# Attention: the table addition and the row maximum as one VectorE operation on negated scores, and the second block's attention in one unrolled pass

## The chip, the cores and the metric

The kernel runs on one core of one Trainium2 chip. The metric is the device time of one execution in microseconds (us); a lower time is better.

## The reference

The program computes two transformer blocks, one after the other, on 512 tokens of width 1024. Only the attention parts matter here.

The first block has four attention variants ("mixers") side by side, each with 4 heads: moba, mla, dil (dilated) and swa (sliding window with a sink). At 512 tokens each comes down to dense causal attention with its own table of biases and masks. The second block has a layer of attention with 16 heads that share 4 key/value heads, with a window of 128 tokens in both directions, 256 context tokens that every query sees, and a learned sink per head. All of them compute, per head and block of 128 queries:

```python
s = einsum('qd,kd->qk', q, k) * scale + bias        # bias: slope * distance, or NEG where masked
s = concat([s, sink])                               # swa and the second block only
p = exp(s - max(s)); p = p / sum(p)                 # softmax over the keys
o = p[..., keys] @ v
```

## The kernel before

`attention_stage` does the attention of all variants. It works in steps: a step `g` is one head `r` and one block `i` of 128 queries (`r, i = divmod(g, q_tiles)`, with `q_tiles` = 4). In the first block step `i` has 128 x (i + 1) key columns, so 128, 256, 384, 512, in one piece. In the second block (`att2`) a step has a piece of 256 context columns without a table, and a piece of 256 or 384 columns with the mask table `band`: 512, 640, 640 and 512 columns for `i` = 0 to 3 (513 and 641 with the sink's column).

Each engine has its own loop over the steps and waits for the others on counters (semaphores):

- TensorE: `score` (L972) writes the scores of a step to PSUM, `turn` (L980) transposes the probabilities 128 columns at a time, `weigh` (L989) multiplies them with v. Its order is `turn(g)`, `score(g + 2)`, `weigh(g - 1)`.
- VectorE: `bias` writes the sink into column 0 of `s` (L1016), copies a piece without a table (L1020) or adds the table to it (L1022), waits for its own additions, and takes the negated row maximum `top` (L1026). `norm` takes the reciprocal of the row's sum and scales the output (L1032, L1034). Its order is `bias(g + 2)`, `norm(g - 1)`.
- ScalarE: `exp` (L1057) computes the exponential of `s` with `top` as its bias, and the row's sum; a copy (L1071) brings the transposed probabilities from PSUM to `pt`. Its order is `exp(g + 1)`, then the copy of `g`. With a row wider than 512 columns there is one PSUM buffer for the transposes (`nt` = 1), so that `turn(g)` waits for the copy of `g - 1`.
- POOL copies the next head's q to `q_now` (L960) as soon as the scores of an earlier head are done.

`s`, `p`, `pt`, `top` and the scores in PSUM have two buffers, one for even and one for odd steps. The first block's stages run their 4 heads in straight code (`turns` = 1). The second block's runs `turns` = 2 times over 8 heads, in a hardware loop; what differs between the passes is addressed through a register, and waits compare with a count that is in a register too:

```python
if turns == 1:
    turn_of_heads(0)
else:
    with eng.Fori(0, turns) as it:
        turn_of_heads(it)
```

Weights come through a ring of 3 slots (`ring`), which SyncE refills as slots come free.

## Time and profile before

| | |
|---|---|
| time, median of 3 runs | 3364.76 us (3358.79 to 3371.78) |
| time of the profiled execution | 3361.15 us |
| its span in the profile | 3359.4 us |
| mean granted clock of TensorE | 0.928 |
| TensorE busy | 2877.3 us (86%) |
| VectorE busy | 1355.0 us (40%) |
| ScalarE busy | 708.1 us (21%) |
| attention of the first block | within 231 to 406 us of the span, four stages with other work between them |
| attention of the second block | 2499.7 to 2681.7 us of the span |

The engine shares are averages over stages with different limits. Attention is about a tenth of the span, so what the change does has to be read from these stages: in each step, which engine stands and which wait ends last. Starts in a timeline are microseconds from the start of the span.

### The profile page before, as it was taken

How to read it: one execution, taken by the hardware profiler on the slowest of the kernel's cores; microseconds unless marked ns; L12 is line 12 of the kernel's file. 1: busy time of each engine (PE TensorE's matmuls, PEld its weight loads, DVE VectorE, ACT ScalarE, POOL GpSimd, SP SyncE). 2: the span in 40 equal slices, each digit the busy share in tenths (PEclk: the TensorE clock that was granted, in tenths of full speed). 3: DMA queues.
4: the chain of work that ended last, by engine and by line, in shares of the span. 5: the costliest groups of instructions: out<-in, count | busy, mean ns of one | idle time of the engine just before them, and what ended most of it. 6: DMA issues, size and time to landing. Idle time of an engine off the chain costs nothing. (4 is left out here: it accounts for less than half of the span.)

```text
span 3359.4 us, 37744 instructions
## 1 busy us (share of the span) xinstructions
PE 2877.3 (86%) x15074; PEld 1775.8 (53%) x15074; DVE 1355.0 (40%) x2470; ACT 708.1 (21%) x1441; POOL 58.2 (2%) x63
## 2 busy tenths in 40 slices
PE   7877879999799999867499999999769977788886
PEld 5645558878466666645263333333558855222222
DVE  4445453333545656565620111112556744011114
ACT  3323423333211010100211111111425521011101
POOL 0010000000000000000000000000020000000000
PEclk9988789999899999978789999999879987999998
DMA  4552242222201010110019999997100010999994
GB/s 186 210 213 76 85 179 79 97 100 88 80 25 48 25 47 25 34 51 0 1 64 368 354 343 339 341 338 285 51 29 1 0 52 11 428 427 428 426 428 202
DMA packets 51905, 551.38 MB, mean 164 GB/s; under 512 B 8711, under 2 KB 16775, under 8 KB 18216
## 3 DMA queue, kind: packets, MB, share of 16 engines
q1 hardware_dynamic: 51752, 549.25, 41.9%
q8 instruction: 107, 1.75, 0.2%
q14 instruction: 46, 0.38, 0.0%
HBM read 547.14 MB, written 2.10 MB: 163 GB/s over the span
## 5 line engine op out<-in xcount | busy, mean ns | idle before, releaser
L2061 PE MATMUL experts_pg_l<-ring,moe_xe_l 128*64 128x512 f32 x1024 | 270.4, 606 | 47.1 <-DMA ring<-in_moe_gu 41.1
L2239 DVE SCALAR_TENSOR_TENSOR residual<-experts_psc,mod,residual 128x512 f32<-128x512 f32 (+1 forms) x138 | 96.2, 699 | 448.6 <-PE experts_psc L2131 372.7
L2061 PE MATMUL experts_pu_l<-ring,moe_xe_l 128*64 128x512 f32 x1024 | 264.3, 594 | 0.0
L2082 PE MATMUL experts_py_l<-ring,experts_turn_l 128*64 128x512 f32 x1024 | 235.4, 602 | 31.1 <-DMA ring<-in_moe_down 29.8
L1399 PE MATMUL hyena_lat<-normed,ring 128*128 128x512 f32 x384 | 173.7, 606 | 15.2 <-PEq L332 13.9
L2082 PEld LDWEIGHTS experts_py_l<-ring,experts_turn_l 128*64 128x64 f32 x1024 | 68.6, 137 | 175.6 <-issue 123.8
L2061 PEld LDWEIGHTS experts_pg_l<-ring,moe_xe_l 128*64 128x64 f32 x1024 | 63.4, 136 | 177.9 <-issue 104.6
L2061 PEld LDWEIGHTS experts_pu_l<-ring,moe_xe_l 128*64 128x64 f32 x1024 | 74.4, 137 | 146.2 <-issue 146.2
L1399 PEld LDWEIGHTS hyena_lat<-normed,ring 128*128 128x128 f32 x384 | 73.7, 194 | 102.3 <-issue 101.2
L473 PE MATMUL w_in_acc<-w_in_w_hi,w_in_h_hi 128*128 128x512 f32 (+1 forms) x272 | 107.1, 394 | 23.7 <-DVE w_in_w_lo L522 22.8
L2231 DVE TENSOR_TENSOR experts_y_low<-experts_py_l,experts_y_whole 64x512 fp32r<-64x512 f32 x64 | 44.0, 688 | 206.3 <-ACT experts_y_whole L2189 112.3
L2220 DVE SCALAR_TENSOR_TENSOR experts_hid_l<-experts_act_l,moe_gate_rows,experts_pu_l 128x512 f32<-128x512 f32 x32 | 23.9, 748 | 245.5 <-ACT experts_act_l L2172 245.5
L1452 PE MATMUL hyena_lat<-hyena_idft_l,hyena_pq 128*128 128x256 f32 x256 | 68.0, 425 | 50.7 <-DVE hyena_pq L1641 50.7
L474 PE MATMUL w_in_acc<-w_in_w_lo,w_in_h_hi 128*128 128x512 f32 (+1 forms) x272 | 106.6, 392 | 0.0
L475 PE MATMUL w_in_acc<-w_in_w_hi,w_in_h_lo 128*128 128x512 f32 (+1 forms) x272 | 106.4, 391 | 0.0
L473 PE MATMUL up_acc<-up_h_hi,up_w_hi 128*128 128x512 f32 x256 | 100.7, 393 | 6.7 <-DVE up_w_lo L522 6.7
L2172 ACT ACTIVATE experts_act_l<-experts_pg_l 128x512 f32<-128x512 f32 x32 | 19.1, 597 | 410.5 <-PE experts_pu_l L2061 410.5
L616 PE MATMUL down_acc<-down_u_hi,down_w_hi 128*128 128x512 f32 x256 | 100.4, 392 | 5.5 <-DVE down_w_lo L643 5.5
L474 PE MATMUL up_acc<-up_h_lo,up_w_hi 128*128 128x512 f32 x256 | 100.3, 392 | 0.0
L475 PE MATMUL up_acc<-up_h_hi,up_w_lo 128*128 128x512 f32 x256 | 100.3, 392 | 0.0
L617 PE MATMUL down_acc<-down_u_lo,down_w_hi 128*128 128x512 f32 x256 | 100.2, 391 | 0.0
L618 PE MATMUL down_acc<-down_u_hi,down_w_lo 128*128 128x512 f32 x256 | 100.1, 391 | 0.0
(525 smaller groups left out, 5261.7 us busy)
## 6 DMA issues: line engine op xcount, KB each, us to landing
ring<-in_moe_gu SPq DMA_DIRECT2D x128, 2048.0 KB, 10.2
ring<-in_moe_down SPq DMA_DIRECT2D x64, 2048.0 KB, 10.9
ring<-in_ada_w SPq DMA_DIRECT2D x24, 2048.0 KB, 9.8
ring<-in_w_up SPq DMA_DIRECT2D x8, 2048.0 KB, 8.1
ring<-in_w_down SPq DMA_DIRECT2D x8, 2048.0 KB, 7.8
ring<-in_w_in SPq DMA_DIRECT2D x4, 2048.0 KB, 15.2
ring<-in_hy_w_in SPq DMA_DIRECT2D x4, 2048.0 KB, 7.8
hyena_win<-table_window SPq DMA_DIRECT2D x4, 1536.0 KB, 7.5
```

Of the source, the lines that this page charges most:

```text
L473: nc.tensor.matmul(bank(i), s_hi, m_hi, start=(k == 0), stop=False)
L474: nc.tensor.matmul(bank(i), s_hi, m_lo, start=False, stop=False)
L475: last = nc.tensor.matmul(bank(i), s_lo, m_hi, start=False, stop=(k == KD - 1))
L616: nc.tensor.matmul(out, w_hi[:, n % B, o], u_hi[:, f % BUFS, :], start=(f == 0), stop=False)
L617: nc.tensor.matmul(out, w_hi[:, n % B, o], u_lo[:, f % BUFS, :], start=False, stop=False)
L618: last = nc.tensor.matmul(out, w_lo[:, n % B, o], u_hi[:, f % BUFS, :], start=False, stop=(f == tiles - 1))
L1399: nc.tensor.matmul(bl[:], w[:, k, o:o + P], h[:, k, 0:SEQ], start=(k == 0), stop=(k == KD - 1))
L1452: last = nc.tensor.matmul(b[:, par * n:(par + 1) * n], pq[:, a, par, f, j * P:(j + 1) * P], table[:, 2 * a + par, k, :], start=(s == 0), s ...
L2061: last = nc.tensor.matmul((pg_l, pu_l)[m][64 * half:64 * half + 64, :], xe_l[:, e, k, :], w[:, kk, m, FH * half:FH * (half + 1)], start=(k ...
L2082: last = nc.tensor.matmul(py_l[64 * half:64 * half + 64, :], turn_l[:, c, i, :], w[:, c, FH * half:FH * (half + 1)], start=(f == 0), stop= ...
L2231: last = nc.vector.tensor_tensor(y_low[rows, e // 2 % 2, FH * half:FH * (half + 1)], py_l[part, :], y_whole[part, :], ALU.subtract)
L2239: nc.vector.scalar_tensor_tensor(out=x[:, d, c0:c0 + n], in0=banks[bank][:, 0:n], scalar=gate[j][:, d:d + 1], in1=x[:, d, c0:c0 + n], op0= ...
```

## The change

The scores are negated: VectorE computes -(score + bias) with one fused operation (`tensor_tensor_reduce`) that also gives the row's minimum, which is the negated maximum, from its stream. The exponential gets the scale -1. A piece without a table is negated by a `tensor_scalar` with the same running minimum. The minimum starts from 1e30, from the negated sink (swa and second block), or from the minimum of the piece before; in the latter two cases VectorE waits for its own earlier instruction on a new counter (`sunk`, `begun`). TensorE's `score` and ScalarE's `exp` now both wait for `topped`, and the counter `biased` is gone. The second block's attention is called with one turn of 16 heads in place of two turns of 8.

```diff
@@ -928,8 +928,10 @@
         q_staged = st.counter("att_q_staged", turns * per)
         held = 2 * q_tiles
         scored = st.counter("att_scored", N + held)
-        biased = st.counter("att_biased", N + 2)
-        topped = st.counter("att_topped", N)
+        joined = [len(p) - 1 for p in pieces]
+        joins = per * sum(joined)
+        begun = st.counter("att_begun", turns * joins)
+        topped = st.counter("att_topped", N + 2)
         raised = st.counter("att_raised", N + 2)
         turned = st.counter("att_turned", N)
         copied = st.counter("att_copied", N + nt)
@@ -937,6 +939,7 @@
         normed = st.counter("att_normed", N + 4)
         summed = st.counter("att_summed", N)
         off = 0 if sink_of is None else 1
+        sunk = st.counter("att_sunk", off * N)
         n_of = [sum(n for _, n, _ in pc) for pc in pieces]
 
         def run(eng, turn_of_heads):
@@ -967,7 +970,7 @@
                     r, i = divmod(g, q_tiles)
                     if i == 0:
                         pe.wait_ge(q_staged.handle, it * per + q_staged.at(r + 1))
-                    pe.wait_ge(biased.handle, it * steps + biased.at(g + 1))
+                    pe.wait_ge(topped.handle, it * steps + topped.at(g + 1))
                     for b, (k0, n, _) in enumerate(pieces[i]):
                         last = nc.tensor.matmul(ps_s[g % 2][:, b * 512:b * 512 + n], q_now[:, r % 2, i * P:(i + 1) * P], k_of(it, r, k0, n), start=True, stop=True)
                     last.then_inc(scored.handle, 1)
@@ -1011,19 +1014,25 @@
                     dve.wait_ge(scored.handle, it * steps + scored.at(g + 1 + held))
 
                     dve.wait_ge(raised.handle, it * steps + raised.at(g + 1))
-                    at = off
+                    at, low = off, 1e30
+                    now = top[:, g % 2:g % 2 + 1]
                     if off:
-                        nc.vector.tensor_scalar(s[:, g % 2, 0:1], sink_of(it, r), 1.0, None, ALU.mult)
+                        low = s[:, g % 2, 0:1]
+                        nc.vector.tensor_scalar(low, sink_of(it, r), -1.0, None, ALU.mult).then_inc(sunk.handle, 1)
+                        dve.wait_ge(sunk.handle, it * steps + sunk.at(g + 1))
                     for b, (k0, n, bs) in enumerate(pieces[i]):
                         src = ps_s[g % 2][:, b * 512:b * 512 + n]
+                        if b:
+                            dve.wait_ge(begun.handle, it * joins + begun.at(r * sum(joined) + sum(joined[:i]) + b))
+                            low = now
                         if bs is None:
-                            last = nc.vector.tensor_copy(s[:, g % 2, at:at + n], src)
+                            last = nc.vector.tensor_scalar(s[:, g % 2, at:at + n], src, -1.0, low, ALU.mult, ALU.min, now)
                         else:
-                            last = nc.vector.tensor_tensor(s[:, g % 2, at:at + n], src, bias_of(it, r, *bs), ALU.add)
+                            last = nc.vector.tensor_tensor_reduce(s[:, g % 2, at:at + n], src, bias_of(it, r, *bs), -1.0, low, ALU.add, ALU.min, now)
+                        if b < joined[i]:
+                            last.then_inc(begun.handle, 1)
                         at += n
-                    last.then_inc(biased.handle, 1)
-                    dve.wait_ge(biased.handle, it * steps + biased.at(g + 3))
-                    nc.vector.tensor_reduce(top[:, g % 2:g % 2 + 1], s[:, g % 2, 0:at], AX_X, ALU.max, negate=True).then_inc(topped.handle, 1)
+                    last.then_inc(topped.handle, 1)
 
                 def norm(it, g):
                     r, i = divmod(g, q_tiles)
@@ -1033,7 +1042,7 @@
                     dve.wait_ge(summed.handle, it * steps + summed.at(g + 1))
                     nc.vector.tensor_scalar(out_of(it, r, i), ps_o[g % 2][:, 0:HD], inv[:, g % 2:g % 2 + 1], None, ALU.mult).then_inc(normed.handle, 1)
 
-                dve.sem_inc(biased.handle, 2)
+                dve.sem_inc(topped.handle, 2)
                 dve.sem_inc(normed.handle, 4)
                 def turn_of_heads(it):
                     bias(it, 0)
@@ -1051,10 +1060,10 @@
             def _(act):
                 def exp(it, g):
                     n = n_of[g % q_tiles] + off
-                    act.wait_ge(topped.handle, it * steps + topped.at(g + 1))
+                    act.wait_ge(topped.handle, it * steps + topped.at(g + 3))
 
                     act.wait_ge(normed.handle, it * steps + normed.at(g + 1))
-                    nc.scalar.activation(p[:, g % 2, 0:n], s[:, g % 2, 0:n], ACT.Exp, bias=top[:, g % 2:g % 2 + 1],
+                    nc.scalar.activation(p[:, g % 2, 0:n], s[:, g % 2, 0:n], ACT.Exp, bias=top[:, g % 2:g % 2 + 1], scale=-1.0,
                                          accum_out=total[:, g % 4:g % 4 + 1]).then_inc(raised.handle, 1)
 
                 act.sem_inc(copied.handle, nt)
@@ -2338,7 +2347,7 @@
             return [(0, CTX, None), (CTX + lo * P, (hi - lo) * P, ((lo - i + 1) * P, (hi - i + 1) * P))]
 
         attention_stage(
-            core, "att2", KV // 2, 2 * REP, MLA_DIM, LT, keys, qT,
+            core, "att2", 1, KV * REP, MLA_DIM, LT, keys, qT,
             lambda it, r, k0, n: kT[:, bass.ds(it * 2 + r // REP, 1), k0:k0 + n].rearrange("p a n -> p (a n)"),
             lambda it, r, kt: cols[:, order[kt], bass.ds(it * (2 * HD) + (D + KV * HD + r // REP * HD), HD)],
             lambda it, r, a, b: band[:, a:b],
```

VectorE, first block, moba: the 384-wide and the 512-wide step of the first head and the normalisation behind them. Names are tiles (`att_moba_s` is the row of scores in SBUF), `ISA` is an operation of the library. Before:

```order
L1022 TENSOR_TENSOR att_moba_s<-att_moba_scores,g_moba_table 128x384 [waits att_raised,att_scored]
L1026 TENSOR_REDUCE att_moba_top<-att_moba_s 128x1 [waits att_biased]
L1022 TENSOR_TENSOR att_moba_s<-att_moba_scores,g_moba_table 128x512 [waits att_raised,att_scored]
L1026 TENSOR_REDUCE att_moba_top<-att_moba_s 128x1 [waits att_biased]
L1032 RECIPROCAL att_moba_inv<-att_moba_total 128x1 [waits att_raised,att_weighed]
L1034 TENSOR_SCALAR mixers_o<-att_moba_out,att_moba_inv 128x64 [waits att_summed]
```

After:

```order
L1031 ISA att_moba_s,att_moba_top<-att_moba_scores,g_moba_table 128x384 [waits att_raised,att_scored]
L1031 ISA att_moba_top 128x1
L1031 ISA att_moba_s,att_moba_top<-att_moba_scores,g_moba_table 128x512 [waits att_raised,att_scored]
L1031 ISA att_moba_top 128x1
L1041 RECIPROCAL att_moba_inv<-att_moba_total 128x1 [waits att_raised,att_weighed]
L1043 TENSOR_SCALAR mixers_o<-att_moba_out,att_moba_inv 128x64 [waits att_summed]
```

The addition has become the fused operation, and the 384- or 512-wide maximum behind it, which waited for `biased`, an instruction that reads out one column and waits for nothing.

VectorE, second block, one 640-wide step in the middle of a head, with `norm` of an earlier step (`att_s` is the row of scores, `swa_o` the output). Before:

```order
L1016 TENSOR_SCALAR att_s<-swa_sink 128x1 [waits att_raised]
L1020 COPY att_s<-att_scores 128x256
L1022 TENSOR_TENSOR att_s<-att_scores,swa_band 128x384
L1025 REGISTER_ALU
L1026 TENSOR_REDUCE att_top<-att_s 128x1 [waits att_biased]
```

After:

```order
L1021 TENSOR_SCALAR att_s<-swa_sink 128x1 [waits att_raised,att_scored]
L1029 TENSOR_SCALAR att_s,att_top<-att_scores,att_s 128x256 [waits att_sunk]
L1031 ISA att_s,att_top<-att_scores,swa_band,att_top 128x384 [waits att_begun]
L1031 ISA att_top 128x1
```

The sink's instruction is now waited for (`sunk`) before the first piece, and the first piece (`begun`) before the second; the maximum over both pieces and the register instruction are gone, a one-column read-out stands at the end.

VectorE, second block, where the loop's pass of 8 heads ends. Before:

```order
L1032 RECIPROCAL att_inv<-att_total 128x1 [waits att_raised,att_weighed]
L1034 ISA [waits att_summed]
L1034 TENSOR_SCALAR swa_o<-att_out,att_inv 128x64
L946 REGISTER_ALU
L946 COMPARE_AND_BRANCH
L949 UNCONDITIONAL_BRANCH
```

After, the same place in the 16 heads (the first step of the ninth head):

```order
L1041 RECIPROCAL att_inv<-att_total 128x1 [waits att_raised,att_weighed]
L1043 TENSOR_SCALAR swa_o<-att_out,att_inv 128x64 [waits att_summed]
L1021 TENSOR_SCALAR att_s<-swa_sink 128x1 [waits att_raised,att_scored]
L1029 TENSOR_SCALAR att_s,att_top<-att_scores,att_s 128x256 [waits att_sunk]
L1031 ISA att_s,att_top<-att_scores,swa_band,att_top 128x256 [waits att_begun]
L1031 ISA att_top 128x1
L1041 RECIPROCAL att_inv<-att_total 128x1 [waits att_raised,att_weighed]
L1043 TENSOR_SCALAR swa_o<-att_out,att_inv 128x64 [waits att_summed]
```

Before, the last steps are normalised with nothing between them and the loop branches back to an empty pipeline; now the ninth head's first step stands between the normalisations of the eighth's last ones.

## Rows read from the trace of the kernel before

**Rows 1.** The page, parts 1 and 2 (40 slices of 84 us)
```profile
PE 2877.3 (86%) x15074; PEld 1775.8 (53%) x15074; DVE 1355.0 (40%) x2470; ACT 708.1 (21%) x1441; POOL 58.2 (2%) x63
...
GB/s 186 210 213 76 85 179 79 97 100 88 80 25 48 25 47 25 34 51 0 1 64 368 354 343 339 341 338 285 51 29 1 0 52 11 428 427 428 426 428 202
```

**Rows 2.** Timeline of moba, second head: start us, length us, engine, line, operation, tiles
```profile
244.46 0.69 DVE L1022 TENSOR_TENSOR att_moba_s<-att_moba_scores,g_moba_table 128x512 f32<-128x512 f32 x1 [0.39 <-PE att_moba_scores L972]
...
245.19 0.69 DVE L1026 TENSOR_REDUCE att_moba_top<-att_moba_s 128x1 f32<-128x512 f32 x1
...
245.91 0.72 ACT L1057 ACTIVATE att_moba_p<-att_moba_s,att_moba_top 128x512 f32<-128x512 f32 x1 [1.22 <-DVE att_moba_top L1026]
...
246.78 0.66 PE L980 MATMUL att_moba_turned<-ident,att_moba_p 128*128 128x128 f32 x4 [1.14 <-ACT att_moba_p L1057]
```

**Rows 3.** Groups of TensorE instructions: busy us, mean ns, idle time before and releaser
```profile
L980 PE MATMUL att_swa_turned<-ident,att_swa_p 128*128 128x128 f32 x40 | 9.4, 342 | 4.1 <-ACT att_swa_p L1057 4.1
...
L980 PE MATMUL att_dil_turned<-ident,att_dil_p 128*128 128x128 f32 x40 | 8.8, 325 | 4.6 <-ACT att_dil_p L1057 4.6
...
L980 PE MATMUL att_moba_turned<-ident,att_moba_p 128*128 128x128 f32 x40 | 7.7, 292 | 5.6 <-ACT att_moba_p L1057 5.6
```

**Rows 4.** Timeline of POOL, second block's attention, one copy a head
```profile
2563.06 0.61 POOL L960 COPY att_q_now<-swa_qT 96x512 f32 x1 [9.76 <-PE att_scores L972]
2573.44 0.61 POOL L960 COPY att_q_now<-swa_qT 96x512 f32 x1 [9.77 <-PE att_scores L972]
2583.80 0.61 POOL L960 COPY att_q_now<-swa_qT 96x512 f32 x1 [9.75 <-PE att_scores L972]
...
2613.18 0.61 POOL L960 COPY att_q_now<-swa_qT 96x512 f32 x1 [9.58 <-PE att_scores L972]
```

**Rows 5.** Timeline of TensorE, second block, most of one head
```profile
2552.35 1.00 PE L989 MATMUL att_out<-swa_cols,att_pt 128*128 x8
2553.60 0.73 PE L980 MATMUL att_turned<-ident,att_p 128*128 128x128 f32 x5 [0.25 <-ACT att_pt L1071]
2554.17 1.03 PE L972 MATMUL att_scores<-normed,att_q_now 96*128 x4
2555.04 1.23 PE L989 MATMUL att_out<-swa_cols,att_pt 128*128 x10
2556.10 0.61 PE L980 MATMUL att_turned<-ident,att_p 128*128 128x128 f32 x4
2556.55 1.24 PE L972 MATMUL att_scores<-normed,att_q_now 96*128 x4
2557.62 1.23 PE L989 MATMUL att_out<-swa_cols,att_pt 128*128 x10
```

**Rows 6.** Timeline, second block, a 640-wide step
```profile
2550.04 0.15 DVE L1016 TENSOR_SCALAR att_s<-swa_sink 128x1 f32 x1 [0.28 <-PE att_scores L972]
...
2550.11 0.42 DVE L1020 COPY att_s<-att_scores 128x256 f32<-128x256 f32 x1
...
2550.44 0.55 DVE L1022 TENSOR_TENSOR att_s<-att_scores,swa_band 128x384 f32<-128x384 f32 x1
...
2551.03 0.82 DVE L1026 TENSOR_REDUCE att_top<-att_s 128x1 f32<-128x641 f32 x1
...
2551.96 0.83 ACT L1057 ACTIVATE att_p<-att_s,att_top 128x641 f32<-128x641 f32 x1 [1.19 <-DVE att_top L1026]
```

**Rows 7.** Groups of instructions on VectorE and ScalarE, for their mean durations
```profile
L1032 DVE RECIPROCAL att_inv<-att_total 128x1 f32<-128x1 f32 x64 | 9.8, 154 | 5.2 <-PE att_out L989 5.2
...
L1124 DVE TENSOR_SCALAR normed<-groups_bank,vec 128x512 f32<-128x512 f32 x8 | 5.7, 748 | 1.3 <-PE groups_bank L1136 1.2
...
L1922 DVE TENSOR_TENSOR_SCAN route_scratch<-route_scratch 16x512 f32<-16x512 f32 x2 | 2.4, 1212 | 0.1
...
L1057 ACT ACT_TABLE_LOAD x3 | 3.8, 1283 | 13.5 <-DVE att_top L1026 11.7 <-DVEq L1037 1.8
```

**Rows 8.** Timeline of the DMA queue (SP) at the last expert stage
```profile
2851.62 16.94 SPq L159 DMA_DIRECT2D ring<-in_moe_gu  x5
```

## The prediction

> **What bounds the kernel now.** I read the page first, then the timelines of the attention stages, then the groups of instructions. The attention stages move almost no data, and the page's last row shows memory traffic at 0 to 2 GB/s in slices 19, 20 and 31 to 32, ahead of the expert stages that stream at 340 GB/s and more [rows 1]. So inside attention the four engines bound each other, and the question is which wait ends last in a step.
>
> In the first block's stages (moba, mla, dil, swa: 4 heads of 4 steps each) TensorE runs `turn`, `score`, `weigh` back to back except before the transposes of the 512-wide step. There it stands 1.14 us, released by ScalarE's exponential, which itself had been idle 1.22 us for VectorE's row maximum [rows 2]. The chain is: scores done, table addition (start 244.46), maximum (245.19), exponential (245.91), transposes (246.78). Addition start to exponential start is 1.45 us, and half of it is the maximum. The waits of the `turned` groups confirm that this repeats: 5.6 us in moba, less in dil (4.6) and swa (4.1), whose early heads wait less [rows 3]; mla reads as moba.
>
> In the second block a head takes 10.37 us (POOL's copies of q, one a head) [rows 4]. TensorE's own work in a head follows from starts in one head [rows 5]: transposes of 5 tiles 0.57 us (2553.60 to 2554.17), of 4 tiles 0.45 (2556.10 to 2556.55); scores of a 512-wide step 0.87, of a 640-wide one 1.07; `weigh` with 5 tiles 1.06, so 0.85 with 4. A head has two of each: 2 x (0.57 + 0.45 + 0.87 + 1.07 + 1.06 + 0.85) = 9.74 us. So TensorE waits only 0.63 us per head. Of that 0.40 lies before the transposes at 2553.60 (the `weigh` ahead of it started at 2552.35 and has 0.85 of work). The row names ScalarE's copy `pt` as the releaser; ScalarE does that copy behind the next exponential, and that one waited 1.19 us for the maximum [rows 6]. So this wait too ends at the VectorE chain, which for a 640-wide step takes 1.92 us from the sink (2550.04) to the exponential (2551.96). The remaining 0.22 is before the other transposes of such a step, and both waits serve one chain: what is waited first is time gained for the second.
>
> The seam of the two loop passes: POOL's copies at 2563.06 and 2583.80 are two heads and 20.74 us apart, those at 2583.80 and 2613.18, with the seam between, two heads and 29.38 us. The refill of the pipeline thus costs **8.64 us** [rows 4].
>
> **The change part by part.**
>
> *Row maximum removed, addition fused.* The order shows that the fused operation is two VectorE instructions, the main one and a read-out of one value, in place of two (addition, maximum). Neither is in the trace of before. Bounds for the main one at 512 columns: not below the plain addition, 0.69 us [rows 2]; at the upper end the scan, the one other row that carries a value from element to element, 1.21 us for 512 [rows 7]. I take the addition's rate: the fused instruction reads the same two inputs and writes the same output, once. Read-out: between 0 and a one-column VectorE instruction, 0.154 us [rows 7]; I take 0.154. Overlap: an instruction behind another with no wait starts about 0.08 us before its end (sink 0.15 long, next start after 0.07; copy 0.42 long, next after 0.33) [rows 6]; a wait on VectorE's own semaphore instead costs 0.04 us beyond the end (addition 0.69 long, maximum 0.73 later) [rows 2]; the handover to ScalarE another 0.03. So a 512-wide step goes from 1.45 us to 0.61 + 0.15 + 0.03 = 0.79, gain **0.65**.
>
> The Trainium skill weighs against this: VectorE: DVE Perf Modes, Rules for kernel authors, advises not to fuse chained VectorE operations for speed and to lower their count. The count in moba stays two for two, so by that rule the first block would gain nothing and the time would come out near 3345. The rows say otherwise, because the second instruction shrinks from 512 columns to one.
>
> *With a pointer operand (swa, second block).* The fused operation starts from the sink or from the running minimum, a per-partition operand. A 512-wide instruction with such an operand takes 0.748 us, without 0.69 [rows 7, 2], so 0.056 more. Before it VectorE now waits for its own sink instruction: 0.15 + 0.04 = 0.19 where 0.07 was. swa, 512 wide: before 0.07 + 1.45 = 1.52, after 0.19 + 0.79 + 0.056 = 1.04, gain **0.48**. Second block, 640 wide: sink 0.19; first piece (256) 0.42 - 0.08 + 0.154 + 0.056 + 0.04 = 0.58; second piece (384) 0.55 - 0.08 + 0.154 + 0.056 + 0.03 = 0.71; sum 1.48 against 1.92, gain **0.44** [rows 6]. Behind VectorE's two new own waits stand only the other pieces of the same step and the normalisation of the step before; VectorE needs 1.48 us and the two short instructions of the normalisation in a step of 2.6 us, so nothing there comes late.
>
> *What TensorE gets back.* moba and mla: four heads, each wait of 1.14 falls by 0.65, plus the first step of a stage. That is 128 wide; the maximum takes 0.13 us per 128 columns (0.69 at 512, 0.82 at 641 [rows 2, 6]), so 0.29 + 0.04 there, and the read-out 0.07 beyond the overlap in its place: 0.26. That makes 4 x 0.65 + 0.26 = 2.9 each. dil: its waits are 1.0 less in total, one head has only about 0.15: 3 x 0.65 + 0.15 + 0.26 = 2.4. swa: two heads 0.48 each, the two early ones have 2 x 1.14 - 1.5 = 0.78 in all, which goes: 1.7. First block **9.9**. The transposes are late next: 0.5 us per head still stays, now with the exponential as its largest part.
>
> Second block: the 0.63 per head falls by 0.44, to 0.19, after which TensorE is nearly the bound: 16 x 0.44 = **7.0**. TensorE's floor caps this part at 16 x 0.63 = 10.
>
> *One unrolled pass.* Removes the seam, **8.6**, one reload of the exponential's table in it (1.28 us long [rows 7], inside the 8.6, not beside it), and the register instructions of each step, which I cost at nothing: they lie in the engines' idle time, and whatever of them is on the path is part of the 0.63 us a head that TensorE waits, so they can add no more than the 0.19 left of it. The negation rides in the exponential's scale, and TensorE's `score` now waits for the finished minimum of two steps back, which `turn` ahead of it has already waited for: both nothing.
>
> *Downstream.* The expert stage takes its stream up when its first slots come free (2851.62) [rows 8] and memory is idle before it [rows 1], so the stages behind shift whole.
>
> Sum: 9.9 + 7.0 + 8.6 = **25.5 us**. The profiled execution took 3361.15 us (span 3359.4, 1.75 around it): 3335.6. It is 3.6 us faster than the median of the runs, 3364.76, so I set 3337, between the two ways of counting (3335.6 and 3339.3).
>
> **The rivals.**
>
> *A. The fused operation runs at half the addition's rate, like the scan.* Then 512 columns take 1.21: 1.21 - 0.08 + 0.154 + 0.03 = 1.31 against 1.45, gain 0.14 in three stages, nothing in swa (1.56 against 1.52): 12 x 0.14 + 3 x 0.13 for the first steps = 2.1. The excess over the addition, 0.52 for 512 columns, is 0.39 for the 384-wide piece of the second block; its chain takes 1.87 against 1.92: 16 x 0.05 = 0.8. With the seam 11.5: **3350** from the profiled time. For it: it carries a value along. Against: only one VectorE row of before does that, and the maximum itself also carries one at the addition's rate (0.69 for 512) [rows 2]. The Trainium skill, Vector Engine (DVE) Microarchitecture Reference, Points that are easy to get wrong, has scalar-tensor-tensor forms with two SBUF sources that are not bf16 run at half throughput, for want of a port for the accumulator; here one source is in PSUM, and no run yet shows such a case. Chance 0.12.
>
> *B. The seam's time is not given back*, because code that runs once has to be fetched where the loop's second pass had it. Then 16.9 remain: **3344**, and with more of it lost up to 3352. Against: the first pass is straight code too and its heads take 10.37 us (2573.44 to 2583.80), as those of the second do [rows 4]. Chance 0.08.
>
> *C. Slower: each fused instruction pays a fixed price for its own program.* The nearest row is ScalarE's table load, 1.28 us [rows 7]. VectorE would then need per step of the second block 1.48 + 1.28 + 0.31 (two instructions of at least 0.154 for the normalisation) = 3.07, 12.3 per head against 10.37: 16 x 1.9 = 31 more, in the first block 16 x (1.28 - 0.65) = 10 more, less 8.6: **3393**. It decides from about 0.8 us per instruction, where 4 x (1.48 + 0.31 + 0.8) reaches 10.37. Nothing in the profile shows such a price on VectorE: four kinds of instruction follow each other in a step with no gap [rows 6]. Chance 0.05.
>
> *D. The waits are another's.* TensorE's waits might end with the q copies or the transposes' bank and not with VectorE; then only the seam comes: **3352**. The chain of starts in moba, each within 0.04 us of what releases it, speaks against it [rows 2]. Chance 0.03.
>
> **How the numbers follow.** Forecast 0.72, A 0.12, B 0.08, C 0.05, D 0.03. Best end of the forecast: read-out and pointer operand free (0.13 more in 14 waits) and the second block at TensorE's floor (3 more): 30 gained, 3331; runs scatter by 2 us below the profiled time. Worst end: A, with the median's 3.6 above the profiled time. Range 3327 to 3353; the forecast's own is 3329 to 3343. A measurement tells 0.5% (16.8 us) from no change. Faster: the forecast and half of B, 0.76. Same: A, D, half of B, and a little of the forecast's rest, 0.19. Slower: 0.05.
>
> **What would show it.** Fused rows: about 0.69 us for 512 columns and a one-column row behind them; at 1.2 us A is right. TensorE's wait before the 512-wide transposes of moba: 0.5 us. Second block: q copies 9.9 us apart with no long gap after the eighth (a gap of some us is B), `turned` waits about 3 us in all. A gap before each fused row is C. I am wrong above all if the fused row is much longer than the addition.

## The result, and the profile after

The changed kernel takes 3325.85 us in the median (3319.89 to 3326.39, 4 runs); before, run beside it, 3366.47 us (3358.79 to 3371.78, 4 runs). The ratio is 0.9877 (95% interval 0.9854 to 0.99): about 1.2% faster. The forecast was 3337 us with a range of 3327 to 3353, so the time lies 1.15 us below the range. From profile to profile, 3361.15 to 3325.78 us (span 3359.4 to 3324.0), the gain is 35.4 us where the sum had 25.5.

Part 1 of the page of after, the row of busy times; it answers to the first row of [rows 1]:

```profile
PE 2864.6 (86%) x15074; PEld 1763.2 (53%) x15074; DVE 1302.5 (39%) x2534; ACT 708.0 (21%) x1440; POOL 58.3 (2%) x63
```

VectorE has 64 instructions more and 52.5 us less to do. TensorE has the same 15074 instructions, but is busy 12.7 us less: equal work in less time is a first sign that the clock had a part.

Timeline of moba's second head in after, the four steps of the chain in [rows 2] (columns: start us, length us, engine, line, operation):

```profile
244.77 0.69 DVE L1031 CUSTOM_DVE_ANT_0 att_moba_s<-att_moba_scores,g_moba_table 128x512 f32<-128x512 f32 x1 [0.60 <-PE att_moba_scores L975]
...
245.39 0.08 DVE L1031 DVE_READ_ACCUMULATOR2_ANT att_moba_top<- 128x1 f32 x1
...
245.51 0.73 ACT L1066 ACTIVATE att_moba_p<-att_moba_s,att_moba_top 128x512 f32<-128x512 f32 x1 [1.09 <-DVE att_moba_top L1031]
...
246.38 0.66 PE L983 MATMUL att_moba_turned<-ident,att_moba_p 128*128 128x128 f32 x4 [0.52 <-ACT att_moba_p L1066]
```

The fused instruction takes 0.69 us for 512 columns, as long as the plain addition did. The read-out takes 0.08 us. From the fused instruction's start to the exponential's it is 0.74 us, against 1.45 before, so a 512-wide step gains 0.71 (forecast 0.65). TensorE's wait before the transposes is 0.52 us (forecast 0.5).

Timeline of after, a 640-wide step of the second block, answering to [rows 6]:

```profile
2543.96 0.15 DVE L1021 TENSOR_SCALAR att_s<-swa_sink 128x1 f32<-128x1 f32 x1 [0.85 <-PE att_scores L975]
2544.15 0.48 DVE L1029 TENSOR_SCALAR_CACHE_REDUCE att_s<-att_scores,att_s 128x256 f32<-128x256 f32 x1
2544.56 0.08 DVE L1029 DVE_READ_ACCUMULATOR att_s<-att_scores,att_s 128x1 f32 x1
...
2544.68 0.62 DVE L1031 CUSTOM_DVE_ANT_0 att_s<-att_scores,swa_band,att_top 128x384 f32<-128x384 f32 x1
...
2545.22 0.08 DVE L1031 DVE_READ_ACCUMULATOR2_ANT att_top<- 128x1 f32 x1
...
2545.34 0.83 ACT L1066 ACTIVATE att_p<-att_s,att_top 128x641 f32<-128x641 f32 x1 [1.19 <-DVE att_top L1031]
```

The chain from the sink to the exponential is 1.38 us, against 1.92 before (forecast 1.48): 0.54 gained per step. The difference from the forecast is the read-out: two of them, 0.08 us each and not 0.154.

Groups of TensorE instructions in after, answering to [rows 3] (the last columns are the idle time before them and its releaser), and POOL's copies of q, one a head, answering to [rows 4]:

```profile
L983 PE MATMUL att_swa_turned<-ident,att_swa_p 128*128 128x128 f32 x40 | 8.1, 303 | 2.9 <-ACT att_swa_p L1066 2.9
...
L983 PE MATMUL att_dil_turned<-ident,att_dil_p 128*128 128x128 f32 x40 | 8.0, 302 | 2.0 <-ACT att_dil_p L1066 1.8
...
L983 PE MATMUL att_moba_turned<-ident,att_moba_p 128*128 128x128 f32 x40 | 7.9, 296 | 2.1 <-ACT att_moba_p L1066 2.1
```

```profile
2506.91 0.61 POOL L963 COPY att_q_now<-swa_qT 96x512 f32<-96x512 f32 x1 [9.75 <-PE att_scores L975]
2516.75 0.61 POOL L963 COPY att_q_now<-swa_qT 96x512 f32<-96x512 f32 x1 [9.22 <-PE att_scores L975]
2526.58 0.61 POOL L963 COPY att_q_now<-swa_qT 96x512 f32<-96x512 f32 x1 [9.22 <-PE att_scores L975]
```

Moba's wait falls from 5.6 to 2.1 us, dil's from 4.6 to 2.0, swa's from 4.1 to 2.9. In swa and dil (2.6 and 1.2 us) this is far less than the time these stages gained (below): the waits alone do not tell it. A head of the second block takes 9.83 us in place of 10.37, from the third to the last copy without a gap.

What the forecast had no term for shows when the first block is cut into its stages. These are windows of before (columns: window and its length, busy time of each engine, granted clock as a share of the full one, DMA share, GB/s): mla's attention, the turning stage (q and k transposed) ahead of dil, dil's attention, the turning stage ahead of swa, swa's attention.

```profile
276.10:308.90 32.80, 25.64 (x152) 20.11 (x153) 21.13 (x64) 15.57 (x48) 2.39 (x5) 0.90 0.13 53
308.90:321.10 12.20, 8.44 (x56) 5.70 (x56) 3.05 (x5) 3.21 (x5) 3.52 (x2) 0.84 0.37 114
321.10:355.10 34.00, 27.85 (x152) 22.07 (x152) 21.23 (x64) 15.58 (x48) 2.39 (x4) 0.83 0.13 53
355.10:369.20 14.10, 10.13 (x48) 5.46 (x48) 3.05 (x5) 1.84 (x3) 2.69 (x2) 0.56 0.32 101
369.20:405.70 36.50, 30.76 (x152) 24.11 (x152) 22.31 (x80) 15.76 (x49) 2.39 (x4) 0.76 0.11 48
```

The same five of after:

```profile
276.40:305.60 29.20, 25.80 (x152) 20.05 (x152) 14.34 (x64) 15.61 (x48) 2.35 (x4) 0.88 0.14 59
305.60:320.80 15.20, 9.53 (x56) 5.89 (x56) 3.05 (x5) 3.21 (x5) 3.54 (x3) 0.78 0.30 94
320.80:350.10 29.30, 25.77 (x152) 20.05 (x153) 14.34 (x64) 15.61 (x48) 2.42 (x5) 0.88 0.15 60
350.10:364.30 14.20, 8.45 (x48) 4.45 (x48) 3.05 (x5) 1.85 (x3) 2.66 (x3) 0.76 0.33 101
364.30:394.50 30.20, 25.78 (x152) 20.13 (x152) 17.57 (x80) 15.63 (x48) 2.39 (x4) 0.89 0.14 58
```

Two things are to be seen. The attention stages gain 3.6, 4.7 and 6.3 us, most where before's mean clock was lowest (0.90, 0.83, 0.76). And the turning stage ahead of dil, in which the change touches nothing, is 3.0 us longer at a lower clock (0.78 against 0.84).

### The profile page after: what moved, and what is told of

It reads as the page before. It is cut to its first block and busy times, and to the rows that moved or that the text cites. A ratio compares the mean times of both kernels' runs of the same rounds, so it can differ in the third digit from the quotient of the medians.

```text
span 3324.0 us, 37445 instructions
## 1 busy us (share of the span) xinstructions
PE 2864.6 (86%) x15074; PEld 1763.2 (53%) x15074; DVE 1302.5 (39%) x2534; ACT 708.0 (21%) x1440; POOL 58.3 (2%) x63
## 5 line engine op out<-in xcount | busy, mean ns | idle before, releaser
L2091 PE MATMUL experts_py_l<-ring,experts_turn_l 128*64 128x512 f32 x1024 | 235.4, 602 | 28.4 <-DMA ring<-in_moe_down 27.1
L2240 DVE TENSOR_TENSOR experts_y_low<-experts_py_l,experts_y_whole 64x512 fp32r<-64x512 f32 x64 | 44.1, 689 | 204.1 <-ACT experts_y_whole L2198 127.1
## 6 DMA issues: line engine op xcount, KB each, us to landing
ring<-in_w_in SPq DMA_DIRECT2D x4, 2048.0 KB, 14.7
```

The lines of the kernel that those rows point to most:

```text
L2091: last = nc.tensor.matmul(py_l[64 * half:64 * half + 64, :], turn_l[:, c, i, :], w[:, c, FH * half:FH * (half + 1)], start=(f == 0), stop= ...
L2240: last = nc.vector.tensor_tensor(y_low[rows, e // 2 % 2, FH * half:FH * (half + 1)], py_l[part, :], y_whole[part, :], ALU.subtract)
```

## The experiments

The runs fall into three groups, each with before run beside it (medians 3363.76, 3363.06 and 3363.82 us). "By spans" compares the one profiled execution of each kernel, "by ratios" the ratios to before. The "stage" of the second block's attention reaches from its first copy of q to the first matmul of the output projection, so some 7 us of turning the outputs are in it. "Time at half clock" below is 2 x (1 - granted clock) x length: of the two levels, 2.4 and 1.2 GHz, the mean tells the share of the lower one.

**1. After once more**, to have it in the same group as the next three.

> The changed kernel once more, timed in five rounds. If the 35 us between the two profiled executions are the change and the further 5 us between the medians are scatter between executions, the ratio to the kernel before comes out at 0.989 to 0.990 and the profiled span again within 5 us of 3324, with heads of 9.84 us in the second block. If code that has moved slows or speeds stages that the change does not touch, those stages differ from before by the same amount as in the first profile of the changed kernel (2 to 5 us faster).

Measured: 3324.75 us (3323.34 to 3328.58), ratio 0.9878 (0.986 to 0.9896). Heads 9.83 us. The result repeats. Before's median here is 3363.76 us, so 39 us are gained by medians, 37.6 by spans. The first block's attention repeats (four stages 117.4 us here, 118.0 in the first profile of after), the second block's too (170.1 and 170.2). But stages that the change does not touch differ between these two profiles: the stretch between the two blocks' attention (472.6 to 2482.4 us here, 473.8 to 2487.2 there, 486.2 to 2499.7 in before) takes 2009.8 us here, 2013.4 there and 2013.5 in before, and what is behind the second block's attention 669.3, 666.6 and 670.7. So a difference of 3 or 4 us between two profiles can be scatter.

**2. Before, its two loop passes written out**, the pipeline still emptied between them.

```diff
-                with eng.Fori(0, turns) as it:
+                for it in range(turns):
                     turn_of_heads(it)
```

> The kernel before, its second block's two passes of 8 heads written out as straight code, with the pipeline still emptied between them. My theory: the seam of 8.64 us is partly the loop itself (VectorE starts 2.9 us after the branch for no wait that is shown, and the exponential's table is loaded again, 1.28 us) and partly the refill. Then 3 to 4.5 us go, and the gap between the eighth and ninth head shrinks from 8.6 to about 4.5 us; heads stay at 10.37 us. Rival: all of it is refill; then nothing changes (ratio 1.000). Rival: straight code has to be fetched; then the second pass starts later and the time rises by some us.

Measured: 3361.08 us (3345.98 to 3370.55), ratio 0.9977 (0.9961 to 0.9993). Timeline of POOL across the seam:

```profile
2580.23 0.61 POOL L960 COPY att_q_now<-swa_qT 96x512 f32<-96x512 f32 x1 [9.69 <-PE att_scores L972]
2590.53 0.61 POOL L960 COPY att_q_now<-swa_qT 96x512 f32<-96x512 f32 x1 [9.69 <-PE att_scores L972]
2605.05 0.61 POOL L960 COPY att_q_now<-swa_qT 96x512 f32<-96x512 f32 x1 [13.91 <-PE att_scores L972]
2623.83 0.61 POOL L960 COPY att_q_now<-swa_qT 96x512 f32<-96x512 f32 x1 [18.16 <-PE att_scores L972]
```

Windows of the same kernel, a head ahead of the seam and the second one behind it:

```profile
2580.20:2590.50 10.30, 10.05 (x73) 8.99 (x71) 7.97 (x24) 5.58 (x13) 0.61 (x1) 1.00 0.01 2
2605.10:2623.80 18.70, 18.70 (x71) 16.41 (x72) 8.18 (x25) 5.95 (x12) 0.57 (x1) 0.50 0.00 1
```

A head takes 10.30 us, not 10.37: the loop's register instructions cost 0.07 us a head, which the prediction had at nothing. Behind the seam TensorE's sequence is quickly back (VectorE's first sink of the second pass starts at 2597.16, no table is loaded): the two copies of q around the seam are 14.52 us apart, in before 19.20 (2583.80 to 2603.00), so 4.7 us of it went, about what was expected, and the rival that all of it is refill is out. But the clock then falls, and a head (71 matmuls in its window, 73 in the other) takes 18.7 us at 0.50 where one took 10.3 at 1.00. So the gap itself was made cheap in this execution and the clock took back more than that. This may be why the kernel's runs spread over 24.6 us; only one of them has a profile.

**3. Before, with one pass of 16 heads**: the second part of the change alone.

```diff
-            core, "att2", KV // 2, 2 * REP, MLA_DIM, LT, keys, qT,
+            core, "att2", 1, KV * REP, MLA_DIM, LT, keys, qT,
```

> The kernel before with one unrolled pass of 16 heads in the second block and the old addition and maximum. My theory: only the seam goes, 8.6 us (ratio 0.9974), heads stay at 10.37 us, TensorE's waits before the transposes stay. Rival: the register instructions of the loop cost something in each step; then heads come out at 10.2 us or less and 11 us or more are gained.

Measured: 3353.02 us (3344.86 to 3357.87), ratio 0.9962 (0.9946 to 0.9977): 10.7 us by medians, 12.8 by the ratio, 10.2 by spans. The second block's stage falls from 189.0 to 176.2 us. Of these 12.8 us, 8.64 are the seam of [rows 4], 16 x 0.07 = 1.1 the register instructions; 3.1 stay, and lie ahead of the third copy of q (21.90 us from the first to it in before, 18.81 here). Two things differ there. The granted clock is 0.84 in before and 1.00 here. And ScalarE's table load, which in the loop starts only behind the wait for the first row maximum, stands at the start of the stage in straight code, where ScalarE has nothing else to do. Before, then this kernel:

```profile
2504.24 1.28 ACT L1057 ACT_TABLE_LOAD   x1 [5.17 <-DVE att_top L1026]
```

```profile
2503.70 1.28 ACT L1057 ACT_TABLE_LOAD   x1 [0.49 <-DVEq L1037]
```

All kernels with this attention in straight code have the load at the start (after at 2487.20 us, 3.44 us ahead of its first exponential), and both with the loop have it behind the wait, in each pass. So the loop put 1.28 us ahead of the first exponential of both passes; the prediction had seen the one at the seam only.

**4. After, in two passes of 8 heads as straight code**: the seam alone, with the fused operation.

```diff
-                with eng.Fori(0, turns) as it:
+                for it in range(turns):
...
-            core, "att2", 1, KV * REP, MLA_DIM, LT, keys, qT,
+            core, "att2", KV // 2, 2 * REP, MLA_DIM, LT, keys, qT,
```

> The changed kernel with its second block's attention in two straight passes of 8 heads. My theory: heads of 9.84 us as in the changed kernel, and a refill of about 4 us between the eighth and the ninth, so 4 us slower than the changed kernel (ratio to before 0.990 where the changed kernel has 0.989). Rival: the fused operation's gain needs the single pass; then heads are slower than 9.9 us.

Measured: 3331.16 us (3324.81 to 3333.52), ratio 0.9894 (0.9878 to 0.991). Timeline of POOL across the seam:

```profile
2562.01 0.61 POOL L963 COPY att_q_now<-swa_qT 96x512 f32<-96x512 f32 x1 [9.22 <-PE att_scores L975]
2574.01 0.61 POOL L963 COPY att_q_now<-swa_qT 96x512 f32<-96x512 f32 x1 [11.40 <-PE att_scores L975]
2584.32 0.61 POOL L963 COPY att_q_now<-swa_qT 96x512 f32<-96x512 f32 x1 [9.69 <-PE att_scores L975]
```

That is 6.4 us more than after once more by medians and 1.2 by spans, around the 4 us expected; heads take 9.83 us, so the rival is out. Emptying and filling the pipeline costs 22.31 - 2 x 9.83 = 2.65 us when the code is straight and the clock stays at the full level. Before's 8.64 us had more in it. Timeline of before at its seam:

```profile
2593.00 0.15 DVE L1016 TENSOR_SCALAR att_s<-swa_sink 128x1 f32 x1 [2.93 <-issue]
...
2594.64 1.28 ACT L1057 ACT_TABLE_LOAD   x1 [6.53 <-DVE att_top L1026]
...
2596.80 1.11 PE L980 MATMUL att_turned<-ident,att_p 128*128 128x128 f32 x4 [5.37 <-ACT att_p L1057]
```

VectorE stood 2.93 us at the loop's end for nothing that the profile shows, ScalarE loaded its table again (1.28 us), TensorE stood 5.37 us, and its first four transposes took 1.11 us where [rows 5] have 0.61 at most: half clock again.

**5. The fused operation in the first block only**; the second block in one pass with addition and maximum, as in experiment 3.

```diff
-        attention_stage(
+        attention_stage_two_ops(
             core, "att2", 1, KV * REP, MLA_DIM, LT, keys, qT,
```

The function called is before's attention stage, unchanged.

> After in the first block; the second block's attention in one unrolled pass with the two operations of before (addition, maximum; exponential waiting for the maximum). It halves the 28.3 us that fusion alone gave (medians 3353.0 of the one unrolled pass alone, 3324.8 of after). If the prediction's own split held, the first block has 9.9 and the second 7.0 of 16.9: scaled to what was found, 3336. By the stages' lengths in the profiles, 16.2 us belong to the first block with the turning stages and 6.1 to the second's attention, the rest is spread: 3332 to 3337. Rival, the first block's gain is no larger than predicted and the excess lies in the second: 3343. Heads of the second block 10.30 us, the first block as in after.

Measured: 3331.28 us (3328.13 to 3333.36), ratio 0.9908 (0.9891 to 0.9924), heads 10.29 us. So fusion gives 3353.02 - 3331.28 = 21.7 us in the first block (22.9 by spans, 18 by ratios) and 6.5 us in the second (4.5 by spans, 10 by ratios, 7.7 by the length of the stage, 177.9 to 170.2). The rival is out: the second block's part is what was predicted (7.0), and the first block's, predicted at 9.9, is twice that.

**6. After, second block without the minimum**: a plain negated copy and addition, no read-outs, no waits of VectorE on itself, exponential with bias 0 and scale -0.001.

```diff
-    last = nc.vector.tensor_tensor_reduce(s[:, g % 2, at:at + n], src, bias_of(it, r, *bs), -1.0, low, ALU.add, ALU.min, now)
+    last = nc.vector.scalar_tensor_tensor(out=s[:, g % 2, at:at + n], in0=src, scalar=-1.0, in1=bias_of(it, r, *bs), op0=ALU.mult, op1=ALU.subtract)
```

> After, with the second block's row minimum left out (plain negated copy and addition, no read-outs, no waits of VectorE on itself); the exponential's bias is 0 and its scale -0.001, so the softmax's values are not those of the reference. Theory 1, TensorE is the bound of a head in after (heads 9.83 us, TensorE's own work 9.74 by rows 5): with VectorE's chain shorter by four read-outs and six own waits per head, heads stay between 9.74 and 9.83 us and the time within 2 us of after. Rival, VectorE's chain still ends the wait of TensorE in a head: heads fall by up to 2 x 0.2 us and the second block by 3 to 6 us, which would say that the read-out is still on the path.

Measured: 3318.61 us (3318.29 to 3319.89), ratio 0.9867 (0.9847 to 0.9886), 6.1 us below experiment 1 by medians, 5.0 by spans, 3.7 by ratios, whose intervals overlap. Timeline of POOL:

```profile
2531.06 0.61 POOL L963 COPY att_q_now<-swa_qT 96x512 f32<-96x512 f32 x1 [9.08 <-PE att_scores L975]
2540.75 0.61 POOL L963 COPY att_q_now<-swa_qT 96x512 f32<-96x512 f32 x1 [9.08 <-PE att_scores L975]
```

A head takes 9.69 us, 0.14 less than with the minimum and 0.05 under the 9.74 that I had summed as TensorE's own work. Over 16 heads that is 2.2 us. The stage is 3.7 us shorter (166.4 against 170.1); the remaining 1.5 lie in its first heads, at half clock for 3.3 us and not 6.8; what makes the rest of the 5.0 is not known. Both expectations missed a little: TensorE bounds a head to within 0.14 us, and the time still fell by more than 2 us. What the minimum still costs in the second block is thus 2 us of heads and no more than that again at the start.

**7. After, the bias table issued last and waited for at the end of the turning stage**, in place of ahead of the first evacuation of the transposes. The same in the second block for band and sinks.

```diff
-                    todo = [(table[:], core.consts["bias"][g])]
+                    todo = []
...
+                def late(sp, tabled, name=name, g=g, table=table, sink=sink):
+                    todo = [(table[:], core.consts["bias"][g])]
...
+                    if late is not None:
+                        late(sp, tabled)
                     core.stream(sp, core.used)
+                    if late is not None:
+                        sp.wait_ge(tabled.handle, tabled.at(16 * late(None, None)))
```

The wait of ScalarE and VectorE ahead of the evacuations is now for the gain vectors alone.

> After, with the bias tables and sinks of the attention stages issued as the last transfers of the turning stages and waited for at the end of these stages, in place of ahead of TensorE's last transposes. Theory 1, the 6.1 us that the two turning stages ahead of mla and dil lost in after are the stand of 3.6 us for the table and the 1.2 GHz stretch behind it: without the stand in the middle, TensorE does all transposes at 2.4 GHz and the stages take 11 to 12.5 us each in place of 14.5 to 15, and the kernel 3 to 9 us less than after. Rival 1, the transfer of the table simply moves to the end: the stand is then at the end of the stage with nothing behind it to run at 1.2 GHz in the stage, but the next attention stage begins at 1.2 GHz: same time within 2 us. Rival 2, the stages are bound by the other transfers: no change.

Measured: 3301.85 us (3301.27 to 3306.45), ratio 0.9816 (0.98 to 0.9832): 23 us below experiment 1 by medians, 21 by ratios, 19.4 by spans against the first profile of after. The forecast of 3 to 9 us was far too low, and so was that of 11 to 12.5 us for a turning stage (8.0 to 9.9). What the stand was, in after's turning stage ahead of mla:

```profile
261.69 0.33 SPq L1229 DMA_DIRECT2D g_mla_table<-table_bias  x1
261.74 1.92 PE L871 MATMUL turn_mla_bank<-ident,normed 128*96 128x128 f32 x16 [0.84 <-PEq L952]
266.54 1.08 ACT L883 ACTIVATE g_mla_kT<-turn_mla_bank 96x512 f32<-96x512 f32 x2 [6.80 <-DMA g_mla_table<-table_bias]
267.28 3.65 PE L871 MATMUL turn_mla_bank<-ident,normed 128*96 128x128 f32 x16 [3.62 <-DVE g_mla_qT L896]
```

The same stage with the table late:

```profile
256.85 0.33 SPq L1242 DMA_DIRECT2D g_mla_table<-table_bias  x1
256.90 3.67 PE L877 MATMUL turn_mla_bank<-ident,normed 128*96 128x128 f32 x32 [0.84 <-PEq L958]
260.50 1.92 PE L273 MATMUL turn_mla_mod_pr<-ring,mod_c_cols 128*32 128x512 f32 x16
```

In after, 16 transposes take 1.92 us, then the evacuations wait for the table (4.85 us from its issue), TensorE stands 3.62 us behind them, and the next 16 transposes take 3.65 us at half clock. With the table late, all 32 take 3.67 us. The table's 4.9 us lie beside this work. The three stages take 8.0, 9.9 and 9.0 us, sum 26.9, at a granted clock of 1.00, in place of 14.7, 15.2 and 14.2, sum 44.1, at 0.76 to 0.78: 17.2 us. Another 4.3 come ahead of moba, 1.4 in the attention stages, and 3.6 are lost in the stage behind swa, whose clock is lower (0.68 against 0.89). This is the fastest kernel of the study. The Trainium skill, DMA: Bandwidth & Descriptors, Rules for kernel authors, says it: issue a transfer early and wait late, so that its fixed cost overlaps. The trace agrees, and adds that the wait cost more than its own length, because half clock stood behind it.

**8. The same edit on before.**

> Before, with the same edit as the kernel above it. Theory 1, before's slow first heads of dil and swa (records at a granted clock of half, heads of 8 us and more in place of 6.7) follow the low clock of the turning stages ahead of them: if these run at 2.4 GHz, dil and swa take 30 to 33 us in place of 34.0 and 36.5, and the kernel 5 to 12 us less than before. Rival, the low clock there is not tied to the stand for the table: stage lengths stay within 1 us of those of before, and the kernel within 3 us.

Measured: 3351.61 us (3345.62 to 3355.65), ratio 0.9963 (0.9949 to 0.9977), 11.5 us below before by medians, 8.9 by spans. Two windows of it, the turning stage ahead of mla and mla's attention:

```profile
264.30:274.60 10.30, 8.92 (x56) 6.97 (x56) 2.91 (x5) 2.96 (x5) 0.00 (x0) 0.76 0.45 143
274.60:310.70 36.10, 30.67 (x152) 24.05 (x152) 21.34 (x64) 15.71 (x48) 2.37 (x4) 0.76 0.11 48
```

The turning stages gain 8.6 us in sum (38.0 to 29.4), but not as theory 1 had it: their clock is 0.76 to 0.84, and swa's attention is as slow as in before (36.4 us at 0.76), mla's slower (36.1 against 32.8). Theory 1 falls, although the kernel's gain lies in its 5 to 12 us: it comes from the shorter turning stages, not from dil and swa (33.3 and 36.4 us against 34.0 and 36.5). The rival's 3 us are out too. A low clock in before's attention does not hang on the stand for the table ahead of it. With the two operations it comes with or without that stand, only at other heads.

**9. After, with 26 more transposes into an unused bank where TensorE stands for the table.**

```diff
+        warm = st.ps("warm", 1) if mod else None
...
+                    if mod and i == 4:
+                        for d in range(26):
+                            nc.tensor.transpose(warm[0:w, d % 4 * P:(d % 4 + 1) * P], src(d % tiles), core.ident[:])
```

> After, with 26 more transposes into a bank that nothing reads, in each turning stage of the first block, where TensorE stands 3.6 us until the table has landed (some 3.1 us of work at the full clock; the transfer itself is as early and as long as in after). Theory 1, the low clock of the second half of the turning stages follows from TensorE's stand: the granted clock stays at 1.0 there, the stages ahead of mla, dil and swa take 11.5 to 12.5 us in place of 14.2 to 15.2, and the kernel 5 to 10 us less than after although TensorE does more. Rival, the clock falls at these places whatever TensorE does before: the stages keep their 14 to 15 us, or grow by the added work, and the kernel takes the same time as after or up to 3 us more.

Measured: 3322.89 us (3319.87 to 3330.2), ratio 0.9884 (0.9863 to 0.9906): no change against after. Timeline, the turning stage ahead of dil:

```profile
305.45 2.27 SPq L1233 DMA_DIRECT2D g_dil_gain<-in_dil_k_g  x1
306.35 3.00 PE L870 MATMUL turn_dil_warm<-ident,mixers_cols 128*64 128x128 f32 x26
...
311.83 2.84 PE L875 MATMUL turn_dil_bank<-ident,mixers_cols 128*64 128x128 f32 x16 [2.48 <-DVE g_dil_qT L902]
```

This one settles less than was hoped. The stand shrank from 4.20 to 2.48 us and the transposes behind it from 3.62 to 2.84; over the three stages the time at half clock fell from 20.3 to 10.7 us. A shorter stand went with a shorter stretch at half clock in each of the three stages. But the granted clock in them is 0.88 and not the 1.0 of theory 1, and the stages are no shorter (44.6 against 44.1 us): the last transfer of the stage ahead of dil landed 1.1 us later (from the table's issue, 6.5 us against 5.4; the issue of the last gain vector took 2.27 us in place of 0.59). Whether the additional transposes caused that was not tried.

## Why the prediction was right, and where it failed

Right: the mechanisms of the three terms and their signs. The fused instruction runs at the addition's rate (rival A is out: 0.69 us, not 1.2), it pays no fixed price (rival C), the seam came back in full (rival B), and the waits were VectorE's (rival D: experiments 3 and 5 find both parts). By its own sum:

| term | predicted | measured | from |
|---|---|---|---|
| first block's attention stages | 9.9 | 18.0 | lengths of the four stages, before 136.0, after 118.0 |
| turning stages between them | 0 | -6.1 | 38.0 to 44.1 |
| second block's attention stage | 7.0 + 8.6 | 18.8 | 189.0 to 170.2 |
| everything else | 0 | 4.7 | the rest of 35.4 |

Of the 4.7 us, 4.1 lie behind the second block's attention (670.7 to 666.6 us), 1.5 of them in the output projection (50.1 to 48.6 us, at a granted clock of 0.84 in its first 10 us before and 1.00 after), and 1.2 in the stage behind swa (25.4 to 24.2 us, 0.84 to 0.89); 0.7 are lost ahead of moba. The second profile of after has only 1.4 of the 4.1 (experiment 1), so at least a part of this term is scatter, and where it could be followed the clock differed; the stages do the same work. Here too "the stages behind shift whole" did not hold.

The step that failed is the one that priced the first block at 9.9 us from durations and waits at the full clock, 0.65 us for each late head and nothing more, together with the sentence "so the stages behind shift whole": these stages gained 18.0 us, 13.5 of them at like clock and some 4.5, by the estimates below, with the clock, and the stages between them lost 6.1. Granted clock appears nowhere in the sum, although half clock filled 41.5 us of before's four attention stages. The prediction even saw the sign of it: it noticed that dil's and swa's "early heads wait less" and took the missing waits as a smaller gain. They waited less because TensorE ran at 1.2 GHz there. Window of before, swa's second head, and below it the same head in after:

```profile
375.60:386.40 10.80, 10.52 (x40) 8.51 (x40) 5.67 (x20) 4.10 (x13) 0.61 (x1) 0.50 0.01 2
```

```profile
370.60:376.90 6.30, 6.30 (x41) 5.45 (x41) 4.51 (x21) 3.88 (x12) 0.62 (x2) 0.87 0.02 4
```

This one head gave back 4.5 us where 1.7 were expected of all four.

How much of the 18.0 is the clock? Stages of the same kind at nearly the same granted clock, with two operations against fused: mla 32.8 at 0.90 against 29.2 at 0.88; moba 31.9 at 0.95 (experiment 3) against 28.4 at 0.94 (experiment 5); swa 33.6 at 0.86 (experiment 2) against 30.8 at 0.86 (experiment 7). That is 3.6, 3.5 and 2.8 us; with dil taken like mla, 13.5 of the 18.0. The other 4.5 are left to the clock by subtraction; that is an argument from these rows, since no run holds the clock fixed. A second estimate comes near it: mla with two operations takes 32.8 us with 6.6 at half clock (before) and 36.1 with 17.3 (experiment 8), so 0.31 us more for each us at half clock; after has 41.5 - 27.1 = 14.4 us less of it, which makes 4.4. Against the 9.9 of the prediction these 13.5 are 3.6 more: 0.6 and 0.7 in moba and mla, 1.2 in dil, 1.1 in swa. In moba the four waits of 1.14 us fell to 0.52, 2.5 us, about as priced; but the other 1.0 of its 5.6 us of waits, in the narrower steps, went too (2.1 is left, four times 0.52), where the prediction had 0.26. The further 1.0 or so is the discount for dil's and swa's early heads.

That the fused kernels spend less time at half clock is not an accident of one execution. The attention stages of the first block, over all profiles:

| operations | kernels | sum of four stages, us | of it at half clock, us |
|---|---|---|---|
| two | before, experiments 2, 3, 8 | 136.0, 139.6, 136.3, 138.7 | 41.5, 51.9, 43.8, 52.7 |
| fused | after, experiments 1, 4 to 7, 9 | 116.6 to 118.0 | 18.9 to 27.1 |

Which moment decides that the clock stays up in a fused stage is not settled. What the rows show is that with the two operations TensorE stands 1.14 us in a step of the 512-wide kind and with one 0.52, and that the stretches at half clock are shorter in every fused profile.

The turning stages' loss can be read off the traces. Before's turning stage ahead of mla, for comparison with after's in experiment 7:

```profile
264.38 3.62 PE L871 MATMUL turn_mla_bank<-ident,normed 128*96 128x128 f32 x16 [0.84 <-PEq L949]
269.86 1.95 PE L871 MATMUL turn_mla_bank<-ident,normed 128*96 128x128 f32 x16 [1.86 <-DVE g_mla_qT L896]
```

In before the first 16 transposes ran at half clock (3.62 us) beside the table's transfer, and TensorE then stood only 1.86 us; in after they are done in 1.92 us, TensorE stands 3.62 us, and what comes behind runs at half clock. The transfer takes 4.8 us either way, so a faster start bought nothing, and the stand cost more. Experiment 7 removes it. But the -6.1 is not a fixed price of fusion. Experiment 3, with the two operations, has after's order ahead of mla (1.92 us, a stand of 3.52, then 3.25 us for the second 16), and its three turning stages take 41.1 us. Over all profiles but those of experiments 7 to 9, which alter these stages, they take 37.2 to 41.1 us with two operations and 41.6 to 44.2 with the fused one: which transposes fall into a stretch at half clock differs from profile to profile with the two operations too.

Smaller terms. The second block's fusion was right (7.0 predicted; 6.5 by medians, 16 x (10.30 - 9.83) = 7.5 by heads). The register instructions, "cost at nothing", cost 1.1. The seam was right as read, though its refill is only 2.65 of the 8.64; a loop-end stand, a table load and half clock are the rest. The remainder of the stage, 18.8 - 7.5 - 1.1 - 8.64 = 1.6, lies in its first heads (21.90 us to the third copy of q in before, 19.73 in after). The clock is not it: both kernels spend about 7 us of that at half clock (0.84 and 0.83). The table load of 1.28 us that the loop puts ahead of the first exponential (experiment 3) would be most of it; no run separates it. TensorE's floor of 9.74 us was 0.05 too high. Last, before's own median moved: the prediction started from 3364.76 and a profile of 3361.15; before's runs, over all groups, reach from 3355 to 3377, twice as far apart as forecast and result.

## What to carry to other kernels

Before pricing a stretch from its waits, read its granted clock: waits that are missing in some heads can be half clock, and a change that closes waits there gains more than they show. Ask of every transfer that is waited for between two pieces of TensorE work whether its wait can stand at the end; here that was worth 23 us, more than half as much as the whole change; on the kernel before the same edit gave 9 to 11 us (experiment 8). When an engine is made faster ahead of a transfer of fixed length, it will stand longer for it.

## What the runs showed of the hardware that was not expected

VectorE's read-out of an accumulated value takes 84 ns (mean of 64 in the second block), about half of a one-column instruction (154 ns), and its successor starts at once. The Trainium skill, VectorE: DVE Perf Modes, Two Vector instructions with no wait between them, says that an operation that also writes out its accumulator is two instructions, and the trace agrees. The fused operation takes 693 ns for 512 columns, 558 for 384, 427 for 256 and 285 for 128 (means of after's first block), with one input in PSUM and one in SBUF; a pointer operand as its starting value adds 57 to 67 ns at every width (752, 620, 484, 352), as the `tensor_scalar` with a minimum does (485 for 256). So the cost that a fused accumulation has here is 84 ns flat, against 0.69 us for a separate maximum of 512.

ScalarE's table load of 1.28 us stands at the start of the second block's attention in every kernel that has it in straight code, and behind the first wait for a row maximum, in each pass, in both kernels that have it in a hardware loop (before and experiment 8).

A head of identical work takes 10.30 us at a granted clock of 1.00 and 18.70 at 0.50 in one execution, and behind a short refill such a stretch came in one kernel (experiment 2) and not in another (experiment 4). A change of 1% in such a kernel can therefore not be told from one profile of each: the stages have to be compared at equal clock, or over several kernels.
